# Unit 0's multiplies take x without rstd; the factor is put in when the banks are emptied

## The reference, cut to what matters

```python
hn = rms_norm(x, norm_g)                    # x * rsqrt(mean(x^2) + eps) * g, per frame
proj = hn @ w_in                            # 1024 -> 3584
h_a, b_a, c_a, z_a, a_b, g_b, z_b = split(proj)
conv_a = causal_dwconv3(c_a * h_a)
out_a = b_a * conv_a * silu(z_a)
v_b = a_b * sigmoid(g_b)
conv_b = causal_dwconv31(v_b) + bias        # 31 taps per channel
out_b = silu(layer_norm(conv_b)) * silu(z_b)
y = rms_norm(x + concat(out_a, out_b) @ w_out, final_norm_g)
```

## Time and profile before

| | us |
|---|---|
| median of three runs (lowest, highest) | 1525.37 (1525.01, 1528.58) |
| the profiled execution, its time | 1525.52 |
| its span in the trace | 1523.7 |
| TensorE busy | 1509.9 (99%) |
| VectorE busy | 1287.2 (84%) |
| ScalarE busy | 586.8 (39%) |
| GpSimd busy | 639.5 (42%) |

### The profile page before, as it was taken

The page is one execution under the profiler, slowest core; times in us unless marked ns, Lnnn a source line. Parts: engine busy times, 40 slices in busy tenths (PEclk is TensorE's granted clock), DMA queues, the critical chain, the costliest instruction groups (busy, mean ns, idle before and its releaser), DMA issues.

```text
span 1523.7 us, 19742 instructions
## 1 busy us (share of the span) xinstructions
PE 1509.9 (99%) x7184; PEld 1331.9 (87%) x7184; DVE 1287.2 (84%) x1295; ACT 586.8 (39%) x973; POOL 639.5 (42%) x563
## 2 busy tenths in 40 slices
PE   9999999999999999999999999999999999999998
PEld 8999999988888888888888888888898778888886
DVE  7699999998877998778788896798898788888875
ACT  5453443343333343323244322223343344444433
POOL 2886879012433331342423331116654544444441
PEclk9999999999999999999999999999999999999999
DMA  7898787699998889998889987776867754555541
GB/s 250 325 368 324 288 324 261 239 312 322 328 330 253 270 274 343 314 321 293 258 267 313 303 243 235 235 224 211 240 221 224 255 183 169 176 191 182 177 152 70
DMA packets 119825, 391.11 MB, mean 257 GB/s; under 512 B 17956, under 2 KB 23076, under 8 KB 116144
## 3 DMA queue, kind: packets, MB, share of 16 engines
q1 hardware_dynamic: 119728, 389.84, 75.4%
HBM read 281.31 MB, written 108.48 MB: 256 GB/s over the span
## 4 chain that ended last, share of the span: by engine, by line
PE 95%; DMA 2%; DVE 2%; issue 1%; ACT 0%; POOLq 0%; SPq 0%; POOL 0%; DVEq 0%; ACTq 0%
PE ps L2197 31%; PE ps L2199 31%; PE ps L2198 31%; DMA w_ring<-weight_forms 2%; PE ps L2324 0%; PE ps L2317 0%; PE ps L2402 0%; PE ps L2406 0%; DMA x_raw<-in_xT 0%; DVE conv_b L1994 0%; DVE w_ring L2017 0%; DVE xf_f L1752 0%; DVE ps L2010 0%; PE ps L2310 0%; PE ps L2208 0%
## 5 line engine op out<-in xcount | busy, mean ns | idle before, releaser
L1954 DVE SCALAR_TENSOR_TENSOR ps<-v,conv_b_taps,ps 128x920 f32<-128x920 f32 (+2 forms) x580 | 630.8, 1088 | 17.8
L2197 PE MATMUL ps<-xf,w_ring 128*128 128x460 f32 (+1 forms) x1624 | 603.0, 371 | 1.8 <-DMA w_ring<-weight_forms 0.9
L2199 PE MATMUL ps<-xf,w_ring 128*128 128x460 f32 (+1 forms) x1624 | 602.6, 371 | 0.0
L2198 PE MATMUL ps<-xf,w_ring 128*128 128x460 f32 (+1 forms) x1624 | 600.8, 370 | 0.0
L2197 PEld LDWEIGHTS ps<-xf,w_ring 128*128 128x128 f32 x1624 | 305.4, 188 | 36.4 <-issue 3.4
L2198 PEld LDWEIGHTS ps<-xf,w_ring 128*128 128x128 f32 x1624 | 305.4, 188 | 34.0
L2199 PEld LDWEIGHTS ps<-xf,w_ring 128*128 128x128 f32 x1624 | 304.9, 188 | 34.2
L1465 ACT ACTIVATE sets<-ps 128x460 f32<-128x460 f32 x168 | 92.7, 552 | 465.7 <-PE ps L2199 465.7
L1275 POOL TENSOR_TENSOR w_ring<-w_ring_f,w_ring 128x512 fp32r<-128x512 f32 x28 | 39.6, 1416 | 229.5 <-ACT w_ring L1495 229.5
L2197 PE MATMUL ps<-out_forms,w_ring 128*128 128x512 f32 x288 | 114.5, 398 | 2.5 <-DVE h_rows_odd L2126 2.0
L1226 POOL TENSOR_TENSOR sets<-sets 128x460 f32<-128x460 f32 x42 | 54.2, 1291 | 140.3 <-ACT sets L1465 140.3
(11 more groups left out here) (215 smaller groups left out, 2088.6 us busy)
## 6 DMA issues: line engine op xcount, KB each, us to landing
w_ring<-weight_forms SPq DMA_DIRECT2D x294, 512.0 KB, 5.6
x_raw<-in_xT SPq DMA_DIRECT2D x32, 460.0 KB, 7.1
weight_forms<-xf SPq DMA_DIRECT2D x7, 2048.0 KB, 13.1
weight_forms<-w_ring SPq DMA_DIRECT2D x7, 2048.0 KB, 12.2
out_weight_forms<-w_ring SPq DMA_DIRECT2D x28, 512.0 KB, 6.7
w_ring_f<-in_w_in SPq DMA_DIRECT2D x56, 256.0 KB, 3.6
xf_f<-in_w_in SPq DMA_DIRECT2D x26, 512.0 KB, 6.1
x_row<-in_x_prompt SPq DMA_DIRECT2D x24, 512.0 KB
```

Of the source, the lines that this page charges most:

```text
L1954: dve.scalar_tensor_tensor(dst, window, wb[:, j, k:k + 1], part, ALU.mult, ALU.add).then_inc(taps_done, 1)
L2197: pe.matmul(out, ahi, bhi, start=(start and x == 0), stop=False, skip_group_check=goes_on)
L2198: pe.matmul(out, ahi, blo, start=False, stop=False, skip_group_check=goes_on)
L2199: mm = pe.matmul(out, alo, bhi, start=False, stop=(stop and x == len(terms) - 1), skip_group_check=goes_on)
```

## The change

1. x of blocks 0 and 1 is multiplied by gain only, inside the splitting itself (ScalarE's copy has a scale, VectorE's subtraction becomes one instruction with a multiply), chunk by chunk. Unit 0's multiplies therefore give sums without rstd.
2. Both blocks' mean squares come from rows of x, loaded and squared on ScalarE; TensorE's two statistics steps, VectorE's adds, and the instruction with gain and rstd are gone. rstd goes to DRAM and comes back spread over the partitions, once into `ca` (periods 0 and 1) and once into ring place 8 (the rest of unit 0).
3. When a bank is emptied in unit 0, VectorE first multiplies it by rstd (`scale_tile`, 128x460, from the bank into `sets`), then ScalarE applies sigmoid or silu in place. The partner tile is still without rstd, so the pair in `sets` is multiplied by rstd once more: on GpSimd for "ga" and "bz" (`times_rstd`), on VectorE for "hc" (in `multiply_in`).
4. Weights of period 0 arrive in four quarters between the pieces of x, with gain ahead of all; ScalarE's and VectorE's lists alternate between x and weights. 46 dummy products stand at the start.
5. Tiles (1,B) and (1,C) use banks 6 and 7, which the taps of conv_b use afterwards; the taps begin in period 2. `tap_quota` gives 94 taps to unit 0 (113 before) and 400 to units 1 to 3 (378 before).
6. The ring for the stored weights leaves out place 8 and takes place 1; the store of a period's weights is in two parts, between which SyncE sends and spreads rstd in period 0.

```diff
     if unit(n) == 0:
-        return {"ga": ["v1s", "v1", "v2"], "hc": ["u1s", "u1", "u2"] + taps,
+        return {"ga": ["v1s", "v1", "v2"], "hc": ["r", "u1s", "u1", "u2"] + taps,
                 "bz": ["b1s", "b1", "b2", "zs", "z"], "zz": []}[kind(n)]
...
     if unit(n) == 0:
-        return {"ga": ["edge", "zero", "carry"], "hc": ["edge", "zero", "carry"]}.get(kind(n), [])
+        return {"ga": ["r", "edge", "zero", "carry"], "hc": ["edge", "zero", "carry"], "bz": ["r"]}.get(kind(n), [])
...
 def tap_quota(n):
     u, g = divmod(n, G14)
-    if n == 0:
+    if n < 2:
         return 0
     if n == III - 1:
         return 7
-    if n in (1, 3):
-        return 8
-    if 1 <= n < 7:
-        return 9
     if g == G14 - 1 and u < 3:
         return 1
+    if u == 0:
+        return 9 if n % 2 else 8
     if g == 0 and u < 4:
         return 3
-    return 10 if u < 4 else 12
+    return 11 if u < 4 else 12
...
-RING = [4, 5, 6, 7, 8, 0]
+RING = [4, 5, 6, 7, 0, 1]
 DEEP = len(RING)
-RAW_E, RAW_F, STAGE = 1, 2, 3
+RAW_E, RAW_F, STAGE = 2, 3, 8
+RSTD_SLOT = 8
...
+        def first_rstd(n):
+
+            rows = ca if n < 2 else ring_f32[:, RSTD_SLOT, :, :].rearrange("p l m -> p (l m)")
+            return rows[:, 0:2 * TB]
+
+        def wait_first_rstd(eng, n):
+            eng.wait_ge(first_rstd_in if n < 2 else first_rstd_kept, 32)
+
+        def first_pair(n):
+            return sets[:, n % 2, QA:QA + 2, :].rearrange("p b t -> p (b t)")
 
         def chunks(g, a, b, f32=False):
 
...
         def bank_of(n, t):
+            if n == 1 and t >= 2:
+                return 4 + t
             return (4 * n + t) % 6 if unit(n) == 0 else (2 * (n - III) + t) % 6
...
-            if kind(n) == "zz" or t in (0, 2):
+            if unit(n) == 0 and (kind(n) == "zz" or t in (0, 2)):
+                eng.wait_ge(first_scaled, SCALED_AT[n, TILE_QUARTER[t]])
+            elif kind(n) == "zz" or t in (0, 2):
...
+            load_first_x(0)
+            load_first_weights(0)
+            load_first_x(1)
+            load_first_weights(1)
+            load_first_x(2)
+            load_first_x(3)
+            load_w(1)
...
+            def spread_first_rstd(n, came):
+                for b in range(2):
+                    sp.dma_start(first_rstd(n)[:, TB * b:TB * (b + 1)],
+                                 first_rstd_rows(b).to_broadcast([P, TB])).then_inc(came, 16)
+
             load_w(2)
-            store_forms(0)
-            store_forms(1)
+            store_weights(0)
+            for b in range(2):
+                sp.wait_ge(x_rstd, b + 1)
+                dst = first_rstd_rows(b)[0].rearrange("(r c) -> r c", c=STAT_COLS)
+                sp.dma_start(dst, x_rs[0:STAT_ROWS, STAT_COLS * b:STAT_COLS * (b + 1)]).then_inc(first_rstd_out, 16)
+            sp.wait_ge(first_rstd_out, 32)
+            spread_first_rstd(0, first_rstd_in)
+            store_sums(0)
+            sp.wait_ge(w_sum, 8)
+            sp.wait_ge(w_lo_w, 4)
+            spread_first_rstd(2, first_rstd_kept)
+            store_weights(1)
+            store_sums(1)
...
+            def times_rstd(n):
+
+                if unit(n) or kind(n) not in ("ga", "bz"):
+                    return
+                wait_first_rstd(pool, n)
+                pool.wait_ge(act_made, ACT_AT[n, "B"])
+                pair = first_pair(n)[:, PAD:]
+                pool.tensor_tensor(pair, pair, first_rstd(n)[:, PAD:], ALU.mult).then_inc(pool_made, 1)
...
+                if unit(n) == 0:
+                    if kind(n) != "hc":
+                        act.wait_ge(first_scaled, SCALED_AT[n, TILE_QUARTER[t]])
+                        made = sets[:, n % 2, QUARTER[TILE_QUARTER[t]], tile_cols(n, t)]
+                        act.activation(made, made, FUNC[kind(n)]).then_inc(act_made, 1)
                     return
                 wait_tile(act, n, t)
...
+            first_x_high(0, range(2))
+            first_weight_high(0)
+            first_x_high(0, range(2, 4))
+            first_weight_high(1)
+            first_x_high(0, range(4, KC))
             weight_high(1, 0)
             weight_high(1, 1)
+            for c in range(STAT_COLS):
+                first_row_square(0, c)
+            first_x_high(1, range(KC))
             weight_high(0, 2)
             weight_high(0, 3)
+            for c in range(STAT_COLS):
+                first_row_square(1, c)
             weight_high(1, 2)
             weight_high(1, 3)
+            evacuate(0, 0)
+            evacuate(0, 2)
 
...
+            def first_x_low(b, ks):
                 for k in ks:
+                    dve.wait_ge(x01_hi, x01_parts(b, k))
+                    high = standing_x(b, 0, k, k + 1)[:, 0, :].bitcast(F32)
+                    dve.scalar_tensor_tensor(standing_x(b, 1, k, k + 1)[:, 0, :], st[:, 2 * b + k // HALF, k % HALF, :],
+                                             gain[:, k:k + 1], high, ALU.mult, ALU.subtract).then_inc(x01_lo, 1)
...
+            def scale_tile(n, t):
+
+                wait_tile(dve, n, t)
+                wait_first_rstd(dve, n)
+                (wait_a_free, wait_d_free, wait_b_free, wait_c_free)[t](dve, n)
+                cols = tile_cols(n, t)
+                rows = first_rstd(n)[:, TB * (t // 2):TB * (t // 2 + 1)]
+                dve.tensor_tensor(sets[:, n % 2, QUARTER[TILE_QUARTER[t]], cols], ps[:, bank_of(n, t), cols], rows[:, cols],
+                                  ALU.mult).then_inc(first_scaled, 1)
 
...
+                if unit(n) == 0 and kind(n) == "hc":
+                    wait_first_rstd(dve, n)
+                    dve.wait_ge(first_scaled, SCALED_AT[n, "B"])
+                    pair = first_pair(n)[:, PAD:]
+                    dve.tensor_tensor(pair, pair, first_rstd(n)[:, PAD:], ALU.mult).then_inc(dve_made, 1)
...
+                if job == 0 and k == 0:
+                    dve.wait_ge(first_scaled, SCALED_AT[1, "C"])
...
+            first_x_low(0, range(2))
+            first_weights_low(0)
+            first_x_low(0, range(2, 4))
+            first_weights_low(1)
+            first_x_low(0, range(4, KC))
             weights_low(1)
-            for h in range(2):
-                first_x_scale(1, range(HALF * h, HALF * h + HALF))
-                first_x_low(1, range(2 * h, 2 * h + 2))
+            first_x_low(1, range(KC))
             dve.wait_ge(ready0, 7)
             dve.tensor_copy(mean_w[:, :], mean_w_f32[:, :]).then_inc(mean_w_ready, 1)
             dve.wait_ge(const_in, 112)
+            scale_tile(0, 0)
+            scale_tile(0, 2)
+            scale_tile(1, 0)
+            scale_tile(1, 1)
             for n in range(1, II):
+                if kind(n - 1) == "zz":
+                    scale_tile(n - 1, 3)
                 taps(TAPS_BEFORE[n])
+                if n == 1:
+                    weights_low(2)
                 empty_banks(n - 1)
-                if n + 1 < II:
+                if n > 1:
+                    scale_tile(n, 0)
+                if 1 < n < II - 1:
                     weights_low(n + 1)
                 finish(n - 1)
+                if n > 1 and kind(n) == "zz":
+                    scale_tile(n, 1)
                 if n == II - 1:
                     form_sum(1, 0)
                     form_low(1, P1)
+                    scale_tile(n, 2)
                     form_sum(1, 1)
                     form_sum(1, 2)
                     form_low(1, P5)
                     form_low(1, P6)
-                taps(TAPS_AFTER[n])
+                    taps(TAPS_AFTER[n])
+                else:
+                    half = len(TAPS_AFTER[n]) // 2
+                    taps(TAPS_AFTER[n][:half])
+                    scale_tile(n, 2)
+                    taps(TAPS_AFTER[n][half:])
...
-                if 4 * n + t >= 6:
+                if n == 3 and t < 2:
+                    wait_evacuated(pe, 0, t)
+                elif n >= 2:
...
-            keep_busy(30)
-            first_statistics()
-            keep_busy(6)
-            first_rstd()
-            keep_busy(9)
-
-            pe.wait_ge(w_lo_w, 2)
+            keep_busy(46)
             for k in range(KC):
```

232 lines of the change are left out of this document (98 added, 134 removed).

## The result

The changed kernel takes 1537.00 us (median of 7 runs, 1533.84 to 1540.17), the kernel before 1528.58 us (7 runs, 1525.01 to 1531.87): ratio 1.0055, 95% interval 1.0042 to 1.0068. It is 8.4 us slower where I had forecast no change.

A forecast was written before the change was run, and what follows sets the result against it. TensorE and VectorE were both taken as full through unit 0, so a head start counts only as far as VectorE follows. 3.55 - 2.25 - 0.7 = 0.6 us gained: predicted 1524.8 us, range 1520.9 to 1530.5.

The forecast's parts named there:

- The start: Ahead of TensorE's first real multiply: it comes at 14.1 instead of 17.65, never starving, a gain of 3.55 us.
- The rstd way: Squares through DRAM to first scaling at 43.5, period 2's high halves near 50: about 2 us of room, costed at nothing.
- every us beyond that room is a us of the end: Rule for period 2's start: lateness past the about 2 us of room lengthens the whole time one for one.
- Rival D: rstd arrives late, TensorE waits at 53.7 for a bank or period 2's weights: about 1526 to 1529; chance 0.10.
- Step 3: VectorE in unit 0: idle between 54 and 64, then full to 305; TensorE waits 2.3 us for P3's half.
- the last pair product: GpSimd's last new product falls into VectorE's subtractions ahead of unit 1: +1.5 us (0 to 2.5).
- the place of the idle time: VectorE idle for period 3's late weights, between 54 and 64: +3.6 us with the second half (0 to 6).
- Step 4: Change to unit 3: three more taps ahead of the form sums make TensorE wait about 0.7 us before P3 near 800.
- rival A: VectorE eats most of the head start at the first changeover: 1524.8 us, range 1522.5 to 1527.5; chance 0.48.

The follow-up runs named there:

- e4: Changed kernel with the seven loads of convolution constants issued behind the store of period 0's sum forms: 1532.55 us, ratio 1.0033.
- e5: e3 and e4 together, constants awaited only before the first convolution product, block 1's squares and rstd earlier, period 2's high halves not awaiting the sum forms' store: 1530.12 us.
- e1: Changed kernel without rstd's round trip through DRAM, unit 0's tiles multiplied by input values instead (outputs not the program's): 1535.83 us, ratio 1.0051.
- e2: Changed kernel with the store of period 0's sum forms moved ahead of the wait for rstd in SyncE's list: 1540.25 us, ratio 1.0079.
- e3: Changed kernel with VectorE making unit 1's first sum and low part in period 13 before scaling tile (13, 0): 1532.59 us, ratio 1.0027.
- e8: Kernel before the change with only the changed kernel's plan of taps (`tap_quota`): 1526.98 us, ratio 0.9992.
- e7: e5 with 10 taps in each of periods 2 to 12 of unit 0, and 10 for 11 later: 1552.54 us, ratio 1.0167.
- f4: e5 with period 2's second four taps ahead of period 3's low weight parts, and block 0's row loads split into 96 and 8 partitions: 1527.18 us, ratio 1.0000.
- i1: f4 with the pair product of the four "hc" periods of unit 0 on GpSimd instead of VectorE: 1525.76 us, ratio 0.9989.
- i3: i1 with two taps of period 3 ahead of the low parts of period 4's weights: 1527.20 us, ratio 0.9997.
- e6: e5 with block 1's x loaded ahead of the rows, all rows squared behind it, and 26 dummies instead of 46: 1533.18 us, ratio 1.0038.
- h2: f4 with fewer taps in unit 0's periods 3 to 5, and 10 taps instead of 11 in periods 47 to 54: 1531.66 us, ratio 1.0021.
- h0: Changed kernel with 50 dummy products of 48 columns on TensorE behind tile (1, 3), during the wait before period 2: 1547.63 us, ratio 1.0135.
- i4: i3 with 38 dummy products instead of 46 at the start: 1529.72 us, ratio 1.0013.
- f5: f4 with 36 dummy products instead of 46 at the start: 1529.49 us, ratio 1.0009.
- g: Changed kernel with each of block 0's four row loads (104 partitions) made as two, of 96 and 8: 1535.25 us, ratio 1.0045.

## Why the prediction was wrong

- **The start** was right: first real matmul at 14.02 (I had 14.1), 3.63 us (3.55), and no starving. That it fits to 0.1 us is partly luck: in the thirteen other profiled executions of kernels with 46 dummies it comes between 13.62 and 14.99.
- **The step that failed is "The rstd way"**, with its end "About 2 us of room, so I cost it at nothing". The chain of it, by terms: last row squared at 39.4 (31.5), rstd out at 40.8 (33), landed at 49.15 (39), first scaling at 53.72 (43.5), sum forms stored at 58.5 (47), period 2's high halves ready for VectorE at 59.8 (50), TensorE's first product of period 2 at 61.1 (53.7). Three things were missed. x of block 1 and the rows came late, since the loads of 104 partitions ran at 187 GB/s where I had put 396 on all of them; ScalarE had eight high parts of x and two of sums ahead of block 1's squares, which I had taken to overlap with the landing; and SyncE was held by the constants until 38.2, with the queue nearly empty (22 GB/s) from 35.6 to 39.4. I had counted the bytes of the queue and not the time that the list stood. e4 shows that this last one is worth at least 3.3 us of the wait, e5 that with ScalarE's order mended too nothing is left of it, e1 and e2 that neither rstd alone nor the order alone is the cause.
- My own rule in that step, "every us beyond that room is a us of the end", was too mild: 7.3 us cost 9.9, with the half clock behind them. The prediction held no term for the clock at all.
- **Rival D** (0.10) named the mechanism and the place. Its 1526 to 1529 was too low, since it reckoned with 3 us lost where the wait was 7.3, and with no half clock.
- **Step 3, VectorE through unit 0**: its sum was made for a TensorE that never stops, and gave 2.3 us of wait at the change to unit 1. In the changed kernel it was not put to the test, because TensorE's own wait gave VectorE time. In e5 it is: VectorE full at 39.5 of 40 us (100 to 140), 4.4 us of waits, 1.7 of them at the change and 2.7 inside the unit. Of its terms, the last pair product was right: the sum under it took 3.90 us, where the same took 2.07 in e3, 1.8 more, and I had 1.5 (in e3 that product falls on another pair of instructions, which takes 4.46 instead of some 4.1). Where I was wrong is the place of the idle time (13.4 us before the first scaling, 2.1 behind it, 7.1 before period 3's weights; I had 3.6 in all from 53.7 on) and the order of work in period 13, of which I had said nothing: two waits of VectorE for a tile inside the run of sums, 2.9 us for TensorE, which e3 removes by order alone.
- **Step 4** had the right place and was mis-sized: 1.6 us at the change to unit 3, not 0.7 (e8, with the plan of taps alone; e7, with one tap less a period, has 0.34).
- Could the forecast have come out with the wait mended? f4 says nearly: 1527.2 beside 1527.9 of the kernel before in the same runs, ratio 1.0000, where rival A had "no change" because "VectorE eats most of the head start". It does: 2.0 us of wait and 1.7 of clock near 110, 1.6 at unit 3, against 4.0 in its trace. No kernel here is faster than before by more than its interval; i1 comes nearest (0.9989, 0.9978 to 1.0000).
- What stays open: why the wait at the change to unit 3 comes in two sizes with one plan of taps, why the half clock lasts 7 products behind one wait and 16 behind another, and whether moving the four products to GpSimd gains anything.

## What to carry to other kernels

When a result becomes due later in a pipeline, follow its whole way through one engine's list of issues, and ask of each thing ahead of it how long the list stands still there, not only how many bytes it moves. Small loads that nobody needs yet belong behind the last urgent one. And on two engines that are both nearly full, a head start for one is worth only what the other can follow: put work into the other's idle time first (e3), look in the new trace whether that idle time is still there (i3), and shorten the start only after.

## What the runs showed of the hardware

- TensorE's granted clock fell to 0.50 (1.2 of 2.4 GHz) behind waits of 7.3 (changed kernel), 4.45 (i3), 4.04 (e4), 3.78 (e6), 2.01 (f4) and 1.87 us (h2), and stayed at 1.00 behind others of 2.9 (e6, at 52.6), 2.02 (h2, at 303) and 1.80 us (e5). At one and the same place, the change to unit 3, it fell behind a wait of 2.3 us in h0, h2 and i4 and not in f5. So the length of a wait alone doesn't tell it, and two kernels with the same waits can differ by the clock's part: 1.7 us in f4, 2.6 in the changed kernel. Behind the long wait before period 2 the half clock lasted 16 products (changed kernel), 15 (e4), 13 (e1), 9 (g), 8 (e3) and 7 (e2).
- In h0 it fell to 0.86 and then 0.50 while TensorE did products of 48 columns one behind the other without a pause, and came back after the real products had run from 71.7 to about 74.
- At the start the profile's clock reads 1.00 throughout, but the dummies come at 7 a us at first and at 10 to 12 a us afterwards. The step comes at about 5 us in f4, 6 in the changed kernel and 8 in h2, and with it the first product at 13.62, 14.02 and 14.99, although the three have the same dummies.
- Loads of 104 partitions of 4 KB came at 187 GB/s each (2.28 us apart) and the same as 96 and 8 partitions at 246 (1.73 apart), while in the kernel before the queue moved 416 and 435 GB/s in 14 to 17 and 17 to 20 us.
- The seven loads of constants, 138 KB together in small pieces, held the issuing engine 24 us (14.2 to 38.2) when they stood behind 9 MB of loads, and 9.2 us (45.5 to 54.7) when they stood behind the last store (e4). hist_b alone, 60 KB, took 3.9 to 4.5 us to issue in both.
